# An opening with x, root and norm row multiplied early, adaLN sums folded to 64 partitions, and an FFN's first activation ahead of a weight split

## What is computed

```
mod = silu(c) @ w_ada[i] + b_ada[i]
sh1, sc1, g1, sh2, sc2, g2, sh3, sc3, g3 = split(mod, 9)
h = modulate(rms_norm(x, norm_pre[i, 0]), sh1, sc1)     # h * (1 + scale) + shift
y = swiglu_ffn(h, w_ffn_in[i, 0], w_ffn_out[i, 0])      # (silu(h @ w_gate) * (h @ w_up)) @ w_out
x = x + 0.5 * g1 * rms_norm(y, norm_post[i, 0])
h = modulate(rms_norm(x, norm_pre[i, 1]), sh2, sc2)
y = hybrid_mixer(h, ...)                                # retention, pooling, SSD, attention, gated and merged
x = x + g2 * rms_norm(y, norm_post[i, 1])
```

## Time and profile before

| | |
|---|---|
| median of 3 runs | 1495.87 us (1495.8 to 1496.01) |
| the profiled execution | 1496.28 us |
| its span | 1494.0 us |
| PE busy | 1476.2 us, 99% |
| weight loads of PE | 1263.1 us, 85% |
| DVE busy | 1148.9 us, 77% |
| ACT busy | 806.7 us, 54% |
| granted clock of PE | 0.999 |
| first square of x starts (ACT) | 5.27 us |
| first product of the kernel starts (L750) | 18.43 us |
| the same of quarters 1, 2 and 3 | 31.20, 43.81 and 56.38 us |
| moved by transfers | 343.45 MB, mean 230 GB/s |

### The profile page before, as it was taken

The page is one execution under the profiler, slowest core; times in us unless marked ns, Lnnn a source line. Parts: engine busy times, 40 slices in busy tenths (PEclk is TensorE's granted clock), DMA queues, the critical chain, the costliest instruction groups (busy, mean ns, idle before and its releaser), DMA issues.

```text
span 1494.0 us, 20534 instructions
## 1 busy us (share of the span) xinstructions
PE 1476.2 (99%) x8011; PEld 1263.1 (85%) x8011; DVE 1148.9 (77%) x1406; ACT 806.7 (54%) x1005; POOL 57.0 (4%) x56
## 2 busy tenths in 40 slices
PE   7999999999999999999999999999999999999998
PEld 5688889998988888888878888899988888888886
DVE  6888877867799878788687787766878988775563
ACT  4544455566563456555465564654746545564553
POOL 0000002200000000000000000040000000000000
PEclk9999999999999999999999999999999999999999
DMA  9899966556777847888768887665567787566652
GB/s 347 284 319 309 326 223 215 171 157 190 219 248 246 285 164 234 259 270 285 243 218 256 278 272 253 187 186 160 171 204 240 244 264 238 176 187 187 189 192 99
DMA packets 203876, 343.45 MB, mean 230 GB/s; under 512 B 18546, under 2 KB 118130, under 8 KB 203780
## 3 DMA queue, kind: packets, MB, share of 16 engines
q1 hardware_dynamic: 185636, 276.08, 57.8%
q10 hardware_dynamic: 18144, 66.07, 13.5%
HBM read 341.05 MB, written 1.05 MB: 229 GB/s over the span
## 4 chain that ended last, share of the span: by engine, by line
PE 97%; DMA 1%; DVE 1%; issue 0%; ACT 0%; POOL 0%; SPq 0%; DVEq 0%; ACTq 0%; POOLq 0%
PE ps L808 12%; PE ps L773 11%; PE ps L766 11%; PE ps L774 11%; PE ps L918 6%; PE ps L919 6%; PE ps L920 6%; PE ps L813 6%; PE ps L1259 5%; PE ps L1260 5%; PE ps L1261 5%; PE ps L852 3%; PE ps L958 1%; PE ps L845 1%; DMA w_raw<-in_w_ffn_in 1%; DVE w_lo L1659 1%
## 5 line engine op out<-in xcount | busy, mean ns | idle before, releaser
L1659 DVE TENSOR_TENSOR w_lo<-w_raw,w_hi 128x1024 fp32r<-128x1024 f32 x480 | 574.4, 1219 | 109.9 <-ACT w_hi L1328 109.8
L1328 ACT ACTIVATE w_hi<-w_raw 128x1024 fp32r<-128x1024 f32 x490 | 504.5, 1051 | 270.4 <-DMA w_raw<-in_w_ffn_out 86.5
L773 PE MATMUL ps<-w_hi,h_both 128*128 128x512 f32 x586 | 231.0, 394 | 0.0
L774 PE MATMUL ps<-w_lo,h_both 128*128 128x512 f32 x586 | 228.3, 390 | 0.0
L766 PE MATMUL ps<-w_hi,h_both 128*128 128x512 f32 x586 | 227.6, 390 | 0.0
L808 PE MATMUL ps<-h_both,w_hi 128*128 128x512 f32 x768 | 206.6, 394 | 0.0
L1259 PE MATMUL ps<-h_both,w_hi 128*128 128x256 f32 x640 | 182.6, 285 | 0.0
L1260 PE MATMUL ps<-h_both,w_hi 128*128 128x256 f32 x640 | 181.0, 283 | 0.0
L1261 PE MATMUL ps<-h_both,w_lo 128*128 128x256 f32 x640 | 181.0, 283 | 0.0
L1675 DVE SCALAR_TENSOR_TENSOR ada_acc<-ada_slab,c_silu,ada_acc 128x1024 f32<-128x1024 f32 x128 | 163.7, 1279 | 7.1 <-DMA ada_slab<-in_w_ada 7.1
L808 PEld LDWEIGHTS ps<-h_both,w_hi 128*128 128x128 f32 x768 | 132.9, 189 | 19.2
(11 more groups left out here) (301 smaller groups left out, 1848.0 us busy)
## 6 DMA issues: line engine op xcount, KB each, us to landing
w_raw<-in_w_ffn_in SPq DMA_DIRECT2D x352, 256.0 KB, 3.7
w_raw<-in_w_in SPq DMA_DIRECT2D x168, 512.0 KB, 3.7
ada_slab<-in_w_ada ACTq DMA_DIRECT2D x126, 512.0 KB, 4.5
w_raw<-in_w_ffn_out SPq DMA_DIRECT2D x88, 512.0 KB, 4.2
ada_slab_first<-in_w_ada SPq DMA_DIRECT2D x16, 512.0 KB, 7.6
w_raw<-in_w_ssm_out SPq DMA_DIRECT2D x16, 512.0 KB, 4.5
w_raw<-in_w_out SPq DMA_DIRECT2D x16, 512.0 KB, 3.4
w_raw<-in_w_pool_out SPq DMA_DIRECT2D x8, 512.0 KB, 3.7
```

Of the source, the lines that this page charges most:

```text
L773: mm(out, hi[:, k, tok(tt)], wh[:, cs], start=(k == 0), stop=False)
L774: mm(out, hi[:, k, tok(tt)], wl[:, cs], start=False, stop=False)
L1328: fn(WH[:, n % N_HI, 0:width], RAW[:, n % N_RAW, 0:width], ACT.Copy).then_inc(w_hi, 1)
L1659: dve.tensor_tensor(WL[:, n % N_RAW, 0:width], RAW[:, n % N_RAW, 0:width], WH[:, n % N_HI, 0:width], ALU.subtract).then_inc(w_lo, 1)
```

## The change

It has three parts. **In the opening** the norm row comes as one partition, ahead of x; PE spreads it over the partitions by two products (banks 2 and 3), and DVE multiplies x by its root and by this row over all 1024 columns (`first_x_pre`) before the scale is known. Per quarter there remain, for each of two token tiles, a product with 1 + scale and an addition of the shift, straight from PSUM. The second broadcast of the norm row goes too. The slabs of quarter 0 come in three pieces (rows 0 to 3, 4 and 5, 6 and 7), and PE takes row 6 instead of 5. ACT's table loads are placed differently. The transposes of quarters 1 to 3 move ahead of the last part (three matmuls) of the chunk before them. **The scale and shift sums**: ACT copies the upper 64 partitions of the accumulator down (`acc_upper_part`), DVE adds them to the lower 64 (`acc_fold`), ACT writes the hi part to partitions 0 to 63 and DVE the lo part to 64 to 127 of one tile, and PE makes one product for each half in place of two. The sum of s = 0 for scale moves from 38 to 41, and the mixers' shift sum from 100 to 101. **The first unit of an FFN**: in step c = 3 (s > 0) ACT and DVE split one chunk less, and DVE does in step 9 of s = 0, so that silu and `act_full` of the next step come ahead of that split.

```diff
@@ constants and helpers
-A_SUM_FFN = 38
+A_SUM_FFN = 41
-SH_SUM_MIX = 100
+SH_SUM_MIX = 101
-    return 1 if (n, t) == (2, 0) else 1 + 3 * (t - 1) + {1: 1, 0: 2, 2: 3}[n]
+    return 1 if (n, t) == (2, 0) else 1 + 5 * (t - 1) + {1: 2, 0: 4, 2: 5}[n]
 def on_pe(q):
-    return (0, 4) if q else (0, 1, 4, 5)
+    return (0, 4) if q else (0, 1, 4, 6)
+def slab_pieces(q):
+    return ((0, 4), (4, 8)) if q else ((0, 4), (4, 6), (6, 8))
@@ SP
             sp.dma_start(CS[:], c_d.rearrange("a (k p) -> p (a k)", p=P)).then_inc(c_landed, 16)
+            sp.dma_start(AROW[0:1, :], norm_pre[0, 0:1, :]).then_inc(first_pre, 16)
...
             first_slabs(0, 1)
-            first_row(0)
+            first_slabs(0, 2)
...
                     first_slabs(q, 1)
-                    if q == 2:
-                        first_row(1)
@@ PE
                 for kk, tt in parts:
                     k = 2 * j + kk
+                    if ahead_of_last is not None and (kk, tt) == parts[-1]:
+                        ahead_of_last()
...
+                ahead = None
+                if s == 0 and c in (2, 5, 8):
+                    def ahead():
+                        first_turn(c // 3 + 1)
+                token_chunk(g, q, unit_banks(s, u), HH, HL, KD, (0, 1), ready, ahead).then_inc(w_used, 1)
...
             def column_sums(n, t, bank):
-                pe.wait_ge(acc_hi, acc_parts(n, t))
-                pe.wait_ge(acc_lo, acc_parts(n, t))
+                pe.wait_ge(acc_act, acc_steps(n, t))
+                pe.wait_ge(acc_dve, acc_steps(n, t))
...
+                    if n != 2:
+                        ins = mm(PS[:, bank + half, :], rounded, ACCH[n][:, cs], start=True, stop=True)
+                        continue
...
-                    if s == 0 and c in (3, 6, 9):
-                        first_turn(c // 3)
...
-            kept_busy(12)
+            pe.wait_ge(first_pre, 16)
+            for half in range(2):
+                ins = mm(PS[:, 2 + half, :], ONE[0:1, 0:1].to_broadcast([1, P]), AROW[0:1, half * HALF:(half + 1) * HALF],
+                         start=True, stop=True)
+            ins.then_inc(first_pre_ps, 1)
+            kept_busy(8)
@@ ACT
+            def acc_upper_part(n, t):
+                act.wait_ge(ada_used.sem, ada_used.at(t, 8 * (PARTS.index(n) + 1)))
+                if n == 0:
+                    act.wait_ge(g_ps.sem, g_ps.at(t - 1, 1))
+                fn(ACCU[n][0:64, :], part(n)[64:128, :], ACT.Copy).then_inc(acc_act, 1)
             def acc_hi_part(n, t):
...
+                act.wait_ge(acc_dve, acc_steps(n, t) - 1)
+                fn(ACCH[n][0:64, :], part(n)[0:64, :], ACT.Copy).then_inc(acc_act, 1)
...
                     if s + 1 < SUBS and c == 35:
+                        acc_upper_part(1, s + 1)
+                    if s + 1 < SUBS and c == 37:
                         acc_hi_part(1, s + 1)
-                    if s + 1 < SUBS and c == 46:
+                    if s + 1 < SUBS and c == 45:
+                        acc_upper_part(0, s + 1)
+                    if s + 1 < SUBS and c == 47:
                         acc_hi_part(0, s + 1)
...
-                    split_to(g + 5)
+                    split_to(g + 4 if s and c == 3 else g + 5)
@@ ACT, mixer
                     if s + 1 < SUBS and c == 95:
                         act.wait_ge(yrl_ok.sem, yrl_ok.at(layer, 1))
+                        acc_upper_part(1, s + 1)
+                    if s + 1 < SUBS and c == 97:
                         acc_hi_part(1, s + 1)
-                    if s + 1 < SUBS and c == 97:
+                        acc_upper_part(0, s + 1)
+                    if s + 1 < SUBS and c == 99:
                         acc_hi_part(0, s + 1)
@@ ACT, start
             act.wait_ge(one_ok, 1)
+            fn(RSSM[:, 0:1], one, ACT.Silu)
             fn(ONER[:], one, ACT.Copy)
             act.wait_ge(c_landed, 16)
             fn(CS[:], CS[:], ACT.Silu).then_inc(c_ok, 1)
+            fn(DUMMY[:], one, ACT.Abs_reciprocal_sqrt)
@@ DVE
+            def first_x_pre(tt):
+                dve.wait_ge(first_pre_ps, 1)
+                chain(dve.scalar_tensor_tensor(Y[:, tt, :].rearrange("p (b n) -> p b n", b=2),
+                                               X[:, tt, :].rearrange("p (b n) -> p b n", b=2), RB[:, tt:tt + 1],
+                                               PS[:, 2:4, :], ALU.mult, ALU.mult))
+            def acc_fold(n, t):
+                dve.wait_ge(acc_act, acc_steps(n, t) - 1)
+                low = part(n)[0:64, :]
+                dve.tensor_tensor(low, low, ACCU[n][0:64, :], ALU.add).then_inc(acc_dve, 1)
...
+                dve.tensor_tensor(ACCH[n][64:128, :], part(n)[0:64, :], ACCH[n][0:64, :], ALU.subtract).then_inc(acc_dve, 1)
@@ DVE, FFN: folds in steps 36 and 46, lo parts in 38 and 48
-                    split_to(g + 4)
+                    split_to(g + 3 if c == (3 if s else 9) else g + 4)
@@ DVE, mixer
                     if s + 1 < SUBS and c == 96:
+                        acc_fold(1, s + 1)
+                    if s + 1 < SUBS and c == 98:
                         acc_lo_part(1, s + 1)
-                    if s + 1 < SUBS and c == 98:
+                        acc_fold(0, s + 1)
+                    if s + 1 < SUBS and c == 100:
                         acc_lo_part(0, s + 1)
```

More of the change, by code:

```diff
@@ L277, in on_pe, with piece_of @@
 def on_pe(q):
-    return (0, 4) if q else (0, 1, 4, 5)
+    return (0, 4) if q else (0, 1, 4, 6)
+def slab_pieces(q):
+    return ((0, 4), (4, 8)) if q else ((0, 4), (4, 6), (6, 8))
+def piece_of(q, k):
+    i = [a <= k < b for a, b in slab_pieces(q)].index(True)
+    return 2 * q + (1 if q else 0) + i
 FIRST_STEPS = [(q, k) for q in range(4) for k in range(8) if k not in on_pe(q)]
@@ L467, in build @@
         ada_landed = [sem(f"ada_landed{s}") for s in range(2)]
-        ada_first = [sem(f"ada_first_landed{s}") for s in range(ADA_FIRST)]
+        ada_first = [sem(f"ada_first_landed{s}") for s in range(9)]
         first_used = sem("ada_first_used")
         first_rows = sem("first_rows_in_psum")
-        first_pre = [sem(f"first_pre_row_landed{s}") for s in range(2)]
+        first_pre = sem("first_pre_row_landed")
+        first_pre_ps = sem("first_pre_row_in_psum")
         late_h = sem("late_h_by_token")
@@ L985, in first_rows_of @@
                 for i, k in enumerate(on_pe(q)):
-                    for n in range(2):
-                        pe.wait_ge(ada_first[4 * q + 2 * n + k // 4], 16)
+                    pe.wait_ge(ada_first[piece_of(q, k)], 32)
                     mm(out, CS[:, k:k + 1].to_broadcast([P, P]), slabs[:, :, k, q * QUARTER:(q + 1) * QUARTER], start=(i == 0),
@@ L1687, in first_steps @@
                     k = FIRST_STEPS[m][1]
-                    for n in range(2):
-                        dve.wait_ge(ada_first[4 * q + 2 * n + k // 4], 16)
+                    dve.wait_ge(ada_first[piece_of(q, k)], 32)
                     if m:
@@ L1702, in first_x_scale @@
                     dve.wait_ge(a_ps.sem, a_ps.at(0, 1))
[L1703 to L1718 removed]
+                scaled_at = []
+                for tt in range(TT):
+                    ins = dve.scalar_tensor_tensor(Y[:, tt, cs], PS[:, 7, QUARTER:2 * QUARTER], 1.0, Y[:, tt, cs], ALU.add,
+                                                   ALU.mult)
+                    scaled_at.append(chain.mark(ins))
+                for tt in range(TT):
+                    chain.need(scaled_at[tt])
+                    dve.tensor_tensor(Y[:, tt, cs], Y[:, tt, cs], PS[:, 7, 0:QUARTER], ALU.add)\
+                        .then_inc(late_h if q else f_ok, 1)
+                if q == 3:
+                    dve.sem_inc(a_ok.sem, 1)
             def first_h_lo(q):
@@ L2206, in _ @@
             dve.wait_ge(c_ok, 1)
-            x_part(0, 0)
-            x_root(0, 0)
+            for tt in range(TT):
+                x_part(0, tt)
+                x_root(0, tt)
+                if tt == 0:
+                    first_x_pre(0)
             first_steps(0)
-            x_part(0, 1)
-            x_root(0, 1)
-            first_x_scale(0)
+            first_x_pre(1)
             first_h_full(0)
```

60 lines of the change are left out of this document (26 added, 34 removed).

## The result

The changed kernel takes 1488.66 us (median of 6 executions, 1487.86 to 1488.93), the kernel before 1495.88 (6 executions, 1495.5 to 1496.05): 7.2 us less, ratio 0.9949 with a 95% interval of 0.9939 to 0.996. The forecast was 1486.9 with a range of 1484.5 to 1490.0: faster, as said, and inside the range, but 1.8 us less was gained than summed up. The profiled execution after took 1487.86 us with a span of 1485.8.

What follows compares the result with a forecast made beforehand. TensorE was taken as the bound, busy 1476.2 of 1494.0 us. Terms -4.7 - 2.5 - 0.25 - 2.1 - 1.0 + 1.5 summed to -9.0 us, giving a median of 1486.9 us, range 1484.5 to 1490.0.

Steps and rivals of the forecast that it cites:

- Part 1: Scale and shift column sums: ten sums lose two matmuls each, 20 at 0.23 us, -4.7 us.
- Part 2: First unit of FFNs: waits for `act_full` vanish in FFNs 2, 3 and 5, -2.5 us; sub-layer 0 gains -0.25 us.
- Part 3: Opening, three quarters: transposes ahead of a chunk's last three matmuls cut PE's wait from 0.85 to 0.16 us, -2.1 us.
- Part 4: Whole opening apart from the moved transposes: -1.0 us, bounds -0.3 and -1.3.
- step g: Opening, PE: the norm row's two fp32 matmuls replace four of twelve fillers, and PE waits for slabs anyway: nothing.
- (c): Opening, DVE: x * root * norm row formed before the scale; ends near 14.7, first scaling there instead of 15.12: -0.4 us.
- (d): Opening, chain behind L991: two scalings and two additions, about 1.65 us: -0.45 us; first product near 17.6.
- Step a: Opening, loads: the norm row issued ahead of x makes x and the first slabs land 0.45 us later.
- Step e: Quarter 1 of the opening: without the broadcast row the slab comes 0.2 to 1.05 us earlier; L991 1.0 us earlier.
- Step f: Opening, ACT: one table load less, one moved ahead of x, taking 1.28 us without drain; roots 0.85 us earlier.
- Part 5: Folded sums' extra DVE and ACT operations: new 0.75 us wait at each of two mixers' shift sums, +1.5 us, bounds 0 and +3.0.
- held by data: Rival: DVE holds quarters 2 and 3 of the opening, moved transposes ask too early; -6.9, 1489.0 us, chance 0.13.

Runs made afterwards that it cites:

- the transposes' run: The changed kernel with the transposes of quarters 1 to 3 back in front of the next chunk: 1490.76 us.
- the last run: The changed kernel with nine early fillers, the norm row's products over 128 rows and DVE's low part of the mixers' shift sum one place forward: 1485.35 us.

## Why the prediction was right, and where it was off

- **Part 1, -4.7.** Right. The page has 20 matmuls fewer; with the sums back, the rest of the kernel is 3.0 us longer, 2.6 without the one wait elsewhere, where 4.6 less the mixers' 2.1 is 2.5.
- **Part 2, -2.5 and -0.25.** Right in place and size. The silu runs at 581.38, ahead of the split at 582.48 that still waits for its transfer, and putting the order back costs 2.3 us where 2.35 were to be expected (2.75 less 0.4). Sub-layer 0 kept 0.27 of its 0.47; 0.22 was summed.
- **Part 3, -2.1.** Right: about 0.16 us is left in each quarter, and the reversal costs 2.1.
- **Part 4, -1.0.** This is where it failed, in step g: "its two fp32 matmuls replace four of the twelve fillers ... Nothing." They are four records of 0.92 us on average, 3.7 us in all, as long as eight or nine fillers at half clock; and being one row high they don't raise PE's clock. In the kernel before, the fillers went over from 0.43 to 0.22 at 7.4; now the level rises between the first and the second rows product (10.62, 11.19). PE, and not DVE, was so the last one at the row: DVE ended its product for the second tile at 14.62, as (c) had it (14.7), but the first scaling, which waits for PE, started at 15.33, 0.6 late. The chain behind it took 1.41 us where (d) has 1.65, which gave 0.25 back, and 0.3 us of the 0.8 for the first product were lost. In other executions it cost more. The same opening gave first products at 17.72, 18.09, 18.51, 18.64, 18.77 and 20.98 in profiled executions. Up to 18.77 they go mainly by how many of the eight rows products fell at half clock, none in the first and two in the last; the 20.98 has five, and a slab that came 0.9 us late. The 0.8 us between the profiled execution and the median fit that; the unprofiled executions themselves have no rows. The prediction had this mechanism among its small losses, "PE's clock after fewer fillers", with a chance of 0.05 and near 1491: it came true at a smaller size. The Trainium skill (page "TensorE: Matmul & The Clock Gate", section "Part 1: The HAM clock gate (the "warmup" mystery)") says that the number of cold matmuls at a start varies from run to run, and the rows here agree, with none to five of eight rows products at half clock.
- I had read the granted clock as 1.00 in each stretch of the earlier trace rows and taken it for full speed in the whole opening. The stretches of the earlier trace rows begin at 12. The view says 1.00 before that too, in the changed kernel from 3 to 7 us:

```profile
3.00:7.00 4.00, 3.63 (x4) 1.16 (x4) 0.15 (x1) 3.25 (x8) 0.46 (x1) 1.00 0.89 338
```

  Under it the products went at half clock, by their pitch. Until the first rise the column told nothing here, the pitch did; the one fall of the level was recorded, as 0.50.
- **Step a.** Mis-sized, without weight: x came 0.15 us later and not 0.45 (its first square at 5.42 against 5.27), and the first slab 0.6 later, if the run with three fillers is taken for its landing (9.97 against 9.40).
- **Step e.** The size was within its bounds, the reason right: quarter 1 came 0.33 us closer to the first product once the transposes' 0.69 is taken off (0.2 was taken), and the broadcast put back costs 0.8 there. Quarter 2 gave 0.24 of it back and quarter 3 gained 0.10, so that part 4 came to -0.7 in place of -1.0: 0.5 by the first product and 0.2 by the quarters.
- **Step f.** ACT's table load started at 3.29, lasted 1.28, and the next activation ran at 4.59: no drain behind it. The row decided rightly. The 2.66 us of the Trainium skill (page "ScalarE: Activation LUTs", section "What ACT_TABLE_LOAD costs") don't hold in this place either.
- **Part 5, +1.5.** Right mechanism, place and engine; mis-sized by 0.6. I stepped DVE's queue in pitches of 1.14, but two of the new steps took 1.25: from the scale's low part to the fold (521.39 to 522.64) and from the split to the shift's low part (528.50 to 529.75). So the low part came 0.2 us later than summed, and PE began 0.14 us after its end (531.11 against 530.97), for which the sum had left 0.1 or less: 1.04 in place of 0.75 in each mixer, 2.1 in all. Why these steps take 1.25 stays open.

By its terms: the span fell by 8.2 us where 9.0 were summed, and the mixers (0.6) and the first product (0.3) account for the difference. The time beyond the span fell by 0.2 (2.3 to 2.1), for which the sum has no term. The other 1.2 us between 8.4 and the median's 7.2 are no term of the sum but the place of the two profiled executions, 0.4 above and 0.8 below their medians; the prediction took the same difference for both. So the 1.8 us missed are 0.8, less 0.2, plus 1.2, and the forecast's nearness to the profiled execution (1487.3 against 1487.86) is by 0.2 us luck. Of the rivals, "no new wait" is out by L984, "held by data" by the transposes' run, a silu that starts late by its row, and the fold never came onto the path in an FFN.

## What to carry to other kernels

Cost a small fp32 product by its records and its pitch at the clock that PE has there, not by how little it computes: four one-row records were 3.7 us and left the clock low. Where a start-up has fillers, see in the pitch where they reach full speed, and don't rely on one-row products to get there. If one place in a side engine's queue is what PE waits for, swap it with the split in front before giving up the saving: that swap was worth 2.2 us, more than the eight matmuls (1.8 us) that the fold had taken out of the mixers.

## What was not expected of the hardware

- Matmuls of one row keep PE busy and yet cost it its clock: in the run with nine early fillers 3.4 us at 0.50 (1.2 GHz) came 1.3 us behind four of them, with no idle time ahead; with 128 rows in the same place none did. This rests on one profiled execution with one row and two with 128 (the last run has the same opening).
- A kernel's first microseconds scatter by up to 3 us between executions, which is as much as a part of this change was worth; most of it is that clock, and 0.9 us a late slab. The kernel before is not free of it: of its 43 executions beside the experiments three took 1498.05 to 1498.2, all others 1495.34 to 1496.9. None of the three was profiled.
- Span less the first product's start is the steadier number: 1467.9, 1467.8 and 1468.1 in the changed kernel and the runs with fillers first and with three fillers, whose first products lie 2.4 us apart. The run with nine early fillers is the exception, with 1468.8 by one wait for `act_full`.
- 64 partitions take DVE 1.21 to 1.22 us and ACT 1.06 for 1024 columns, the same as 128 (1.22 and 1.05).
